# Down projection with the tokens on the output partitions, the gate folded into the weight slabs and the residual added in the banks

## The reference, cut to what matters

```python
D_MODEL = 1024; SEQ = 512; D_FF = 2816; EPS = 1e-6

def _rmsnorm(x, w):
    xf = x.astype(jnp.float32)
    y = xf * lax.rsqrt(jnp.mean(xf * xf, axis=-1, keepdims=True) + EPS)
    return (y * w.astype(jnp.float32)).astype(x.dtype)

def _swiglu(h, w_gate, w_up, w_down):
    return jnp.matmul(jax.nn.silu(jnp.matmul(h, w_gate)) * jnp.matmul(h, w_up), w_down)

# after both token mixers, per layer; g2 is one value per channel, from c and w_mod:
#   x = x + g1 * mixers(...)
#   x = x + g2 * swiglu(modulate(rmsnorm(x, norm2_w), sh2, sc2), w_gate, w_up, w_down)
# and behind the last layer:
#   return rmsnorm(x, final_norm_w)
```

## Time and profile before

| what | us |
| --- | --- |
| median of three launches | 1856.88 |
| lowest and highest | 1856.56, 1857.29 |
| span of the profiled execution, first to last instruction | 1855.5 |
| median less this span | 1.4 |
| PE busy in the span | 1671.6 (90%) |
| DVE, ACT, POOL busy | 895.9, 662.5, 663.6 |

### The profile page before, as it was taken

The page is one execution under the profiler, slowest core; times in us unless marked ns, Lnnn a source line. Parts: engine busy times, 40 slices in busy tenths (PEclk is TensorE's granted clock), DMA queues, the critical chain, the costliest instruction groups (busy, mean ns, idle before and its releaser), DMA issues. The chain is left out here.

```text
span 1855.5 us, 22101 instructions
## 1 busy us (share of the span) xinstructions
PE 1671.6 (90%) x7747; PEld 1314.7 (71%) x7747; DVE 895.9 (48%) x1333; ACT 662.5 (36%) x913; POOL 663.6 (36%) x345
## 2 busy tenths in 40 slices
PE   6689989988988998898998899897999799999997
PEld 1577767677676776776767777674787588888885
DVE  1476287277357537618735754764345533333002
ACT  4435423343342442433334334242233422322113
POOL 1434225224233432522423343340344244444441
PEclk9899989999999998999999999998999899999999
DMA  8122122122211212212121222120332233333221
GB/s 312 50 57 80 46 69 71 54 63 62 68 45 57 79 57 62 74 45 71 54 68 56 67 58 68 57 79 23 113 101 80 68 91 91 101 91 99 94 90 68
DMA packets 212667, 140.82 MB, mean 76 GB/s; under 512 B 4641, under 2 KB 197793, under 8 KB 212641
## 3 DMA queue, kind: packets, MB, share of 16 engines
q1 hardware_dynamic: 212640, 140.47, 25.3%
HBM read 138.36 MB, written 2.10 MB: 76 GB/s over the span
## 5 line engine op out<-in xcount | busy, mean ns | idle before, releaser
L251 POOL TENSOR_TENSOR wlo<-raw,whi 128x1024 fp32r<-128x1024 f32 x202 | 502.8, 2489 | 1100.9 <-ACT whi L247 1100.9
L257 PE MATMUL bank<-hx_hi,whi 128*128 128x512 f32 x1184 | 496.9, 420 | 50.2 <-DVE acc_b L885 29.6
L258 PE MATMUL bank<-hx_lo,whi 128*128 128x512 f32 x1184 | 475.4, 402 | 0.0
L259 PE MATMUL bank<-hx_hi,wlo 128*128 128x512 f32 x1184 | 474.5, 401 | 0.0
L247 ACT ACTIVATE whi<-raw 128x1024 fp32r<-128x1024 f32 x202 | 213.3, 1056 | 308.1 <-PE bank L259 287.1
L257 PEld LDWEIGHTS bank<-hx_hi,whi 128*128 128x128 f32 x1184 | 230.7, 195 | 113.0 <-issue 58.6
L259 PEld LDWEIGHTS bank<-hx_hi,wlo 128*128 128x128 f32 x1184 | 230.6, 195 | 51.3
L258 PEld LDWEIGHTS bank<-hx_lo,whi 128*128 128x128 f32 x1184 | 231.6, 196 | 49.4 <-issue 5.0
L257 PE MATMUL bank<-hc_hi,whi 128*128 128x256 f32 x384 | 116.5, 303 | 30.0 <-DVE modt L896 30.0
L810 ACT ACTIVATE E<-E 128x1024 f32<-128x1024 f32 x56 | 59.3, 1059 | 218.0 <-DVE E L932 217.9
L258 PE MATMUL bank<-hc_lo,whi 128*128 128x256 f32 x384 | 115.4, 300 | 0.0
(11 more groups left out here) (266 smaller groups left out, 2589.8 us busy)
## 6 DMA issues: line engine op xcount, KB each, us to landing
raw<-in_w_in_dram SPq DMA_DIRECT2D x104, 512.0 KB, 3.9
mraw<-in_w_mod_dram SPq DMA_DIRECT2D x32, 512.0 KB, 4.0
raw<-in_w_ffn_gate_dram SPq DMA_DIRECT2D x22, 512.0 KB, 3.8
raw<-in_w_ffn_up_dram SPq DMA_DIRECT2D x22, 512.0 KB, 3.8
raw<-in_w_ffn_down_dram SPq DMA_DIRECT2D x22, 512.0 KB, 3.3
wm<-in_w_mod_dram SPq DMA_DIRECT2D x4, 2048.0 KB, 8.5
raw<-in_w_proj_ret_dram SPq DMA_DIRECT2D x16, 512.0 KB, 3.7
xt<-in_x_dram SPq DMA_DIRECT2D x2, 2048.0 KB, 12.9
```

The source lines that it names most:

```text
L251: pool.tensor_tensor(wlo[slot][:, :], raw[slot][:, :], whi[slot][:, :].bitcast(F32), ALU.subtract).then_inc(lo_done, 1)
L257: pe.matmul(dst, whi[slot][:, cols], pick(pair[0]), start=start, stop=False)
L258: pe.matmul(dst, whi[slot][:, cols], pick(pair[1]), start=False, stop=False)
L259: return pe.matmul(dst, wlo[slot][:, cols], pick(pair[0]), start=False, stop=stop)
```

## The change

It turns the down projection round and reorders what lies behind it. In the new code:

- The stationary operand of a down matmul is a piece of `g` (128 channels by the 128 tokens of block t), the moving operand is half a slab (512 output channels). Bank 2t+half holds 128 tokens by 512 channels. The number of matmuls of this kind stays 528.
- The gate is folded in: DVE multiplies each of the 22 slabs by `g2b`, the gate on all partitions (`scale_slab`), before ACT and POOL split it. `g2b` is made once: DVE writes eight diagonal blocks `diag`, two fp32 matmuls by ones spread them, ACT copies them.
- The residual is added in the banks: `residual(b)` puts `x1` into bank b with four fp32 matmuls by the identity ahead of the down matmuls. Banks 4 to 7 get theirs before the gate and up products, banks 0 to 3 inside slab 0.
- There are six slots for converted slabs (the two of before, and four in `hx`, which is free after the gate and up products) and four for raw ones (two in `x1`, free after the residual).
- Slabs 0 to 15 run over all four token blocks each. The last six are held back and used block by block: block 0 with slabs 16 to 21, then block 1, 2, 3.
- The final normalisation goes by token block. ACT squares both banks of a block with a sum along the row, then Ln and Exp on 128 x 1 numbers, DVE multiplies the banks by the final weight (`fwb`, one broadcast load of 512 KB) and by the row's factor, and SP stores both pieces. No matmul by ones and no transposition follows the down matmuls.
- The last turn of gate and up stands outside the loop on ACT and DVE, and so do all down steps on all engines.

```diff
+        g2b, fwb = [acc[1][:, 2 * i:2 * i + 2, :].rearrange("p c l -> p (c l)") for i in range(2)]
+        ssq, row_rstd = sb(tail, "ssq", [P, NT, 3]), sb(tail, "row_rstd", [P, NT])
+        n_slots, k_rows = 6, FT - 6
+        d_hi, d_lo = ([w[i][:, :] for i in range(2)] + [hx[j][:, 2 * i:2 * i + 2, :].rearrange("p c l -> p (c l)") for i in range(4)]
+                      for j, w in enumerate((whi, wlo)))
+        stage = [raw[i][:, :] for i in range(2)] + [x1[:, 2 * i:2 * i + 2, :].rearrange("p c l -> p (c l)") for i in range(2)]
...
+        def stage_of(k):
+            return k if k < 2 else k - 2 if k < 4 else (k - 2) % 4
...
+            diag = sb(st, "diag", [P, D])
...
-        BEFORE_DOWN = [4 + FT // 2] * 4 + [6, 6, 3, 2]
+        BEFORE_DOWN = [4 + FT // 2] * 4 + [6, 6, 4, 3]
...
+                after(sp, mrg_done, KT)
+                sp.dma_start(fwb, a["final_norm_w"].unsqueeze(0).to_broadcast([P, D])).then_inc(fw_in, 16)
...
-                with sp.Fori(0, FT // 2) as i:
-                    for j in range(2):
-                        load_slab(sp, j, w_down[:, bass.ds(i * 2 + j, 1), :], D, i * 2 + (SD + j))
...
+                for k in range(FT):
+                    if k < 2:
+                        sp.wait_ge(lo_done, SD + k + 1)
+                    elif stage_of(k) < 2:
+                        sp.wait_ge(lo_done, SD + k - (2 if k < 4 else 4) + 3)
+                    elif k < 6:
+                        sp.wait_ge(down_used, 1)
+                    else:
+                        sp.wait_ge(lo_done, SD + k - 4 + 3)
+                    s, n = landed(k)
+                    sp.dma_start(stage[stage_of(k)], w_down[:, k, :]).then_inc(s, 16)
+                for t in range(NT):
+                    for half in range(2):
+                        ns = slice(half * 512, (half + 1) * 512)
+                        sp.wait_ge(fin_ready, 2 * t + half + 1)
+                        sp.dma_start(out[0, t * P:(t + 1) * P, ns], y_out[:, t, ns]).then_inc(y_stored, 16)
...
-                with pool.Fori(0, (SD + FT - S0 - 2) // 2) as i:
+                with pool.Fori(0, (SD - S0) // 2) as i:
                     for slot in range(2):
                         split_lo(pool, i * 2 + (S0 + 2 + slot), slot)
+                for k in range(2, FT):
+                    pool.wait_ge(hi_done, SD + k + 1)
+                    pool.tensor_tensor(d_lo[k % n_slots], stage[stage_of(k)], d_hi[k % n_slots].bitcast(F32), ALU.subtract).then_inc(lo_done, 1)
...
+                pe.wait_ge(diag_ready, KT)
+                for half in range(2):
+                    after(pe, free[6 + half], 2)
+                    pe.matmul(bank(6 + half), ones[:, 0:P], diag[:, half * 512:(half + 1) * 512], start=True, stop=True).then_inc(full[6 + half], 1)
...
+                def residual(b):
+                    t, half = b // 2, b % 2
+                    after(pe, free[b], BEFORE_DOWN[b])
+                    for c in range(4):
+                        pe.matmul(bank(b)[:, c * P:(c + 1) * P], x1[:, 4 * half + c, t * P:(t + 1) * P], ident[:, :], start=(c == 0), stop=False)
+                for b in (4, 5, 7, 6):
+                    residual(b)
...
-                def down(k, slot, first_, last):
+                def down(k, t):
+                    slot = k % n_slots
                     pe.wait_ge(lo_done, k + (SD + 3))
                     after(pe, g_done, k + 1)
-                    for n in range(KT):
-                        if first_:
-                            after(pe, free[n], BEFORE_DOWN[n])
-                        m = passes(pe, bank(n), slot, n * P, g, lambda t: t[:, k, :] if isinstance(k, int) else one(t, k), first_, last)
-                        if last:
-                            m.then_inc(full[n], 1)
-                    if not last:
-                        m.then_inc(down_used, 1)
-                for k in range(2):
-                    down(k, k, k == 0, False)
-                with pe.Fori(1, FT // 2 - 1) as i:
-                    for j in range(2):
-                        down(i * 2 + j, j, False, False)
-                for k in range(FT - 2, FT):
-                    down(k, k % 2, False, k == FT - 1)
-                after(pe, free[0], BEFORE_DOWN[0] + 1)
-                for n in range(KT):
-                    pe.wait_ge(sq_ready, KT + n + 1)
-                    m = pe.matmul(bank(0), ones[:, 0:P], sqs[n % 4][:, :], start=(n == 0), stop=(n == KT - 1))
-                    m.then_inc(sq_summed, 1)
-                for half in range(2):
-                    pe.wait_ge(fin_ready, 4 * (half + 1))
+                    for half in range(2):
+                        b = 2 * t + half
+                        ts, ns = slice(t * P, (t + 1) * P), slice(half * 512, (half + 1) * 512)
+                        if k == 0 and b < 4:
+                            residual(b)
+                        pe.matmul(bank(b), g[0][:, k, ts], d_hi[slot][:, ns], start=False, stop=False)
+                        pe.matmul(bank(b), g[0][:, k, ts], d_lo[slot][:, ns], start=False, stop=False)
+                        m = pe.matmul(bank(b), g[1][:, k, ts], d_hi[slot][:, ns], start=False, stop=(k == FT - 1))
+                        if k == FT - 1:
+                            m.then_inc(full[b], 1)
+                    return m
+                for k in range(k_rows):
                     for t in range(NT):
-                        b = OUT_BANK[half][t]
-                        after(pe, free[b], BEFORE_DOWN[b] + (2 if b == 0 else 1))
-                        for k in range(4):
-                            m = pe.transpose(bank(b)[:, k * P:(k + 1) * P], x1[:, 4 * half + k, t * P:(t + 1) * P], ident[:, :])
-                        m.then_inc(full[b], 1)
+                        m = down(k, t)
+                    m.then_inc(down_used, 1)
+                for t in range(NT):
+                    for k in range(k_rows, FT):
+                        down(k, t)
...
+                after(act, mrg_done, KT)
+                for half in range(2):
+                    act.wait_ge(full[6 + half], 3)
+                    act.activation(g2b[:, half * 512:(half + 1) * 512], bank(6 + half), ACT.Copy).then_inc(free[6 + half], 1)
...
+                def ffn(i, last):
...
+                        if last and j >= 2:
+                            act.wait_ge(w_scaled, j - 1)
                         split_hi(act, i * 2 + (HALF0 + 12 + j // 2 + 1), j % 2)
                 with act.Fori(0, FT // 2 - 1) as i:
-                    for j in range(2):
-                        act.wait_ge(down_used, i * 2 + (j + 1))
-                        split_hi(act, i + (HALF0 + 12 + FT + 1), j)
-                for n in range(KT):
-                    after(act, free[n], BEFORE_DOWN[n] + 1)
-                    if n >= 4:
-                        act.wait_ge(sq_summed, n - 3)
-                    act.activation(sqs[n % 4][:, :], x1[:, n, :], ACT.Square).then_inc(sq_ready, 1)
-                act.wait_ge(sq_summed, KT)
-                rstd(0, None)
+                    ffn(i, False)
+                ffn(FT // 2 - 1, True)
+                for k in range(2, FT):
+                    slot = k % n_slots
+                    if k >= n_slots:
+                        act.wait_ge(down_used, k - n_slots + 1)
+                    act.wait_ge(w_scaled, k + 1)
+                    act.activation(d_hi[slot], stage[stage_of(k)], ACT.Copy).then_inc(hi_done, 1)
                 for t in range(NT):
-                    act.wait_ge(full[OUT_BANK[0][t]], BEFORE_DOWN[OUT_BANK[0][t]] + 2)
-                    act.activation(outs[0][t], bank(OUT_BANK[0][t]), ACT.Copy).then_inc(y_copied[0], 1)
-                for t in (1, 3):
-                    act.wait_ge(full[OUT_BANK[1][t]], BEFORE_DOWN[OUT_BANK[1][t]] + 2)
-                    act.activation(outs[1][t], bank(OUT_BANK[1][t]), ACT.Copy).then_inc(y_copied[0], 1)
+                    act.activation(row_rstd[:, t:t + 1], eps[:, 0:1], ACT.Ln)
+                    for half in range(2):
+                        b = 2 * t + half
+                        act.wait_ge(full[b], BEFORE_DOWN[b] + 1)
+                        act.activation(nn[b % 4][:, :], bank(b), ACT.Square, accum_out=ssq[:, t, half:half + 1]).then_inc(squared, 1)
+                        act.drain()
+                        if half == 0:
+                            act.activation(ssq[:, t, 2:3], ssq[:, t, 0:1], ACT.Identity, bias=eps[:, 0:1], scale=1.0 / D)
+                    act.activation(row_rstd[:, t:t + 1], ssq[:, t, 1:2], ACT.Ln, bias=ssq[:, t, 2:3], scale=1.0 / D)
+                    act.drain()
+                    act.activation(row_rstd[:, t:t + 1], row_rstd[:, t:t + 1], ACT.Exp, scale=-0.5).then_inc(row_ready, 1)
...
+                for k in range(KT):
+                    dve.tensor_scalar(diag[:, k * P:(k + 1) * P], ident[:, :], modt[:, 40 + k, 0:1], None, ALU.mult).then_inc(diag_ready, 1)
...
+                def scale_slab(k):
```

(21 more changed lines are left out.)

62 lines of the change are left out of this document (25 added, 37 removed).

## The result

The changed kernel took 1838.41 us (median of four runs, 1832.62 to 1841.57), the kernel before 1857.09 beside it: ratio 0.9896, 95% interval 0.9873 to 0.9919. The direction was right. The two profiled spans differ by 15.9 us; the forecast had 13.9. That these are close is chance. What the change does is worth 12.0 to 12.5 us, and the rest is a part of the program that it doesn't touch. Of the kernel before, one run beside the experiments took 5723.56 us and is left out of all that follows.

A forecast was written before the change was run, and what follows sets the result against it. PE alone bounds the down projection; at the end engines wait for one another. Terms -14.8 - 3.4 + 3.6 + 0 + 0.9 - 0.2 = -13.9 take the span from 1855.5 to 1841.6; forecast 1843.0 us, range 1840.0 to 1848.5.

The forecast's parts named there:

- the pace of down: 528 down matmuls: start 0.2267 us apart instead of 0.2331, since hx's tile or the converted slabs move instead of g; -3.4 us.
- the step from the sum to the time: Whole kernel: -13.9 us takes the profiled span from 1855.5 to 1841.6; the median lies 1.4 above, so 1843.0 us.
- The end: From the end of the last down matmul: normalisation by token block and store take 7.3 us in place of 22.1; -14.8 us.
- The rival with 0.3: Down matmuls: the pace stays at 0.233 and the operand swap gives nothing; 1846.4 us, chance 0.3.
- The residual in banks 0 to 3: Inside slab 0 of down: sixteen fp32 matmuls in four sets of 0.89 us, fully on the path; +3.6 us.
- The residual in banks 4 to 7: Between sum of squares and first gate product: DVE and ACT set that product's end, so 0; +2.2 us if the clock stays down.
- The rival of a clock that stays down: Over the first gate product: clock stays down because PE idles between tiles; +2.2 us, 1845.2 us, chance 0.1.
- The gate on all partitions: Between the transposes and w_out: two fp32 matmuls spreading the gate delay w_out; +0.9 us, between 0 and 1.8.
- The last turn: Last turn of gate and up: no table load of its own, so PE pauses less; -0.2 us.
- The slabs: Down slabs: load, scaling, copy and subtraction keep ahead of PE's 5.44 us per slab; 0, slabs 0 and 1 some tenths.
- The slab rival: Down: scaling waits for POOL, slabs become the bound and PE waits 1.3 us on some 20; 1868 us, chance 0.05.

The follow-up runs named there:

- after_again: The changed kernel run once more with no edit, in more rounds beside the kernel before: 1840.71 us, ratio 0.9921.
- by_slab: The changed kernel with its last six slabs used slab by slab like the others: 17.8 us from the last down matmul to the end.
- g_padded: The changed kernel with 384 unused bytes ahead of mrg and g, so g begins at 448 modulo 512: down 122.27 us, w_out to its sum 48.24.
- all_shifted: The changed kernel with 384 unused bytes ahead of mrg and g and 128 ahead of hx, all tiles at 64 modulo 512: down 122.28 us.
- before_padded: The kernel before with 480 unused bytes ahead of mrg and g, which then begin at 448 modulo 512: down 119.45 us instead of 122.97.
- before_aligned: The kernel before with 96 unused bytes ahead of mrg and g, so they begin where they do in the changed kernel: down 122.96 us, pace still 0.2333.
- no_residual: The changed kernel without the residual matmuls of banks 0 to 3 inside slab 0: down stretch 122.70 us, against 126.29 with them.
- no_scaling: The changed kernel with DVE's scaling of each down slab cut to one column: down 125.25 us, the same as with full scaling.

## Why the prediction was right and where it was wrong

Two steps failed. One is a term of the sum, the pace of down. The other is the step from the sum to the time, and it alone put the time below the range: the forecast gave the 1396 us ahead of the tail no spread of their own.

Measured between the profiles of before and after_again, which start the tail within 0.2 us of each other, the change gives -12.0 us; the forecast had -13.9. (With the first profile of the changed kernel it is -12.5: its sum to gate is 0.8 shorter and its loop of gate and up 0.4 longer.) The terms below add up to it: -15.5 - 0.5 + 3.6 + 0.8 - 0.4 = -12.0.

**The end** (-14.8 forecast, -15.5 measured). Right, and inside its bounds of 6.5 to 9 us: 6.6 from the end of the last matmul (1833.0) to 1839.6, forecast 7.3; the difference is nearly all the store, 2.7 instead of 3.3. by_slab shows that the order by token block is the larger half of it.

**The pace of down** (-3.4 forecast, -0.5 measured): this step failed. The prediction saw two paces at one clock, and put the difference on which tile moves. It took the one reading that gave a gain. g_padded, all_shifted and before_padded show the cause: the starts of the stationary and the moving tile against each other, modulo 512 bytes (or 256). The swap leaves that as it was, 448 against another byte, so it could not give the step to 0.2267. What it did give is 0.0009 us a matmul; before_aligned has `g` at the same byte and stays at 0.2333, so that is not the start of `g` alone, and its cause is open. The rival with 0.3 was right in size. The Trainium skill (TensorE: Matmul & The Clock Gate, Back-to-back issue gap) gives for a matmul by itself a distance made of columns and clock alone; by it the swap changes nothing, which is close to what came out. But no run shows its 216 ns, and three paces at one clock and one width, 0.2267, 0.2324 and 0.2333, don't fit a rule of columns and clock.

**The residual in banks 0 to 3** (+3.6 forecast): +3.6, by no_residual. Right: four such matmuls take 0.81 here and 0.89 in the earlier trace rows, but the matmul behind them pays 0.09.

**The residual in banks 4 to 7** (0 forecast, up to +2.2): 0.0. From the sum of squares to the first gate product it is 7.33 us in after_again and 7.32 before, and the first 24 gate matmuls take 9.54 and 9.55. The rival of a clock that stays down didn't occur: in after_again the granted clock is 0.53 from 1458.0 to 1461.2, while PE makes the residual, and 1.00 from 1461.2 to 1473.0.

**The gate on all partitions** (+0.9 forecast, 0 to 1.8): +0.65, and 0.14 more from w_out itself: its first matmul, behind the fp32 one, takes 0.64 to the next instead of 0.33, and the others go at 0.2324 instead of 0.2333. PE's rows of after for it:

```profile
1401.74 1.96 PE L1179 MATMUL bank<-diag,ones 128*128 128x512 f32 x4 [0.90 <-ACT x L1240]
1403.13 0.80 PE L257 MATMUL bank<-mrg_hi,whi 128*128 128x512 f32 x1
1403.77 0.39 PE L258 MATMUL bank<-mrg_lo,whi 128*128 128x512 f32 x1
```

PE waited 0.90 for ACT's copy, as the prediction had it, and the two matmuls took 1.39 together instead of 1.78.

**The last turn** (-0.2): -0.4 (the last 96 matmuls of gate and up take 21.91 us before and 21.53 in the changed kernel). Right in kind.

**The slabs** (0): right. no_scaling moves nothing. The slab rival (1868 us) had its mechanism right, DVE and POOL exclude each other, as the one-column product shows, but with both in turns a slab takes 3.34 us, and PE uses one in 5.6.

**From the sum to the time: this step failed too.** The forecast took the profiled run of before as the start, and the small spread of three runs (1856.56 to 1857.29) as the spread of the kernel. Both were luck: later runs of before go from 1844.5 to 1864.0. The range held only the unknowns of the change, and none for 1396 us of program that run at a clock granted differently each time. With the true -12.0 the forecast would have been 1844.9; 1838.41 is 6.5 lower, of which 3.3 can be seen in the profiled run ahead of the tail, and the other three runs have clocks of 0.957, 0.960 and 0.962. So two errors of opposite sign stand in the result: the pace term, 2.9 us too good, and the part ahead, for which the forecast had nothing and which was some 6 us quicker than in the first runs of before. Of these 6 us a trace shows only the 3.3.

What stays open: why the clock is granted differently from run to run; whether the step that counts is 512 or 256 bytes; and why, with unequal starts, w_out gains 0.0009 us a matmul by the shift in before_aligned and down doesn't.

## What to carry to other kernels

Cost a change from a landmark just ahead of it to the end, and give the untouched part its own spread; three runs that agree are not a spread. Take what one edit is worth from the shortest stretch that holds it: over the longer one the residual seemed to cost 3.2 us, over the shorter one 3.6. When two products run at different paces at one clock, compare where their tiles start before crediting which operand moves; an unused tile of 384 bytes gave 4.0 us here, a third of what the whole change did. When a normalisation must follow the last matmul, order the last matmuls by what the normalisation needs (10.7 us here), and keep table loads out of it.

## What the runs showed of the hardware that was not expected

- Matmuls with 512 columns on a 128x128 tile start 0.2267 us apart when the stationary and the moving tile begin at the same byte modulo 512 (448 and 448, 64 and 64), and 0.2324 to 0.2333 apart when one begins at 448 and the other at 64 or 480, at full granted clock; 256 in place of 512 is not ruled out; the height of the tile in SBUF made no difference (109504 or 138688).
- The mean granted clock of a program on one core differs from run to run, 0.950 to 0.963 over all runs, and the span is some 1.6 us shorter for each 0.001 more; before spreads over 19 us (1844.5 to 1864.0).
- A VectorE product of one column beside GpSimd's subtractions took 1.5 us on average and up to 2.36, against 0.16 where GpSimd stood still; that of 1024 columns took 3.0, against 1.21.
- The first matmul of 512 columns behind a set of fp32 matmuls starts 0.32 us ahead of the next instead of 0.23 (1707.37 to 1707.69 in the changed kernel).
